# A delta-rule stage beside neighbourhood attention: diagonal blocks turned by TensorE, state update moved to ScalarE and GpSimd

## The reference, cut to what matters

```python
gamma = jnp.exp(jnp.where(lower, gc[..., :, None] - gc[..., None, :], -jnp.inf))
a_mat = jnp.where(strict, jnp.einsum('bhncd,bhnsd->bhncs', kb, k) * gamma, 0.0)
t_mat = a_mat + jnp.eye(C, dtype=f32)
u = triangular_solve(t_mat, v * beta[..., None], ...)
qk = jnp.einsum('bhncd,bhnsd->bhncs', q, k) * gamma
def step(S, inp):
    v_new = u_n - jnp.einsum('bhck,bhkv->bhcv', w_n, S)
    o = jnp.einsum('bhck,bhkv->bhcv', qd, S) + jnp.einsum('bhcs,bhsv->bhcv', qk_n, v_new)
    S = S * gl[..., None, None] + jnp.einsum('bhck,bhcv->bhkv', kd, v_new)
    return S, o
```

## Time and profile before

| | us |
|---|---|
| median of 3 runs | 3741.64 |
| lowest, highest | 3738.85, 3743.60 |
| the profiled execution | 3740.74 |
| its span | 3738.8 |
| TensorE busy in the span | 3666.4 |
| the delta stage, 371 to 720 us of the span | 349 |
| TensorE busy in that stage | 302.65 |

### The profile page before, as it was taken

One profiled execution on the slowest core, in us unless ns is written; L12 is line 12 of the kernel. 1 busy time (PEld: TensorE's weight loads), 2 busy tenths in 40 slices (PEclk: granted clock), 3 DMA queues, 4 the chain that ended last, 5 costly groups with the idle time before them and its releaser, 6 DMA issues.

```text
span 3738.8 us, 50657 instructions
## 1 busy us (share of the span) xinstructions
PE 3666.4 (98%) x21121; PEld 2968.1 (79%) x21121; DVE 2148.3 (57%) x3262; ACT 1579.8 (42%) x2544; POOL 81.4 (2%) x85
## 2 busy tenths in 40 slices
PE   8999888899999999999999999999999999999998
PEld 5887677778888878888788889888787788788887
DVE  5641678775345578757588564366655266555333
ACT  5451666634333444435353452333443333434333
POOL 0000121000000000000000000000000000000000
PEclk9999999999999999999999999999999999999999
DMA  5124321324322222222222222222222222223222
GB/s 198 46 74 107 83 58 40 116 91 108 111 91 95 94 81 80 90 96 91 89 80 91 94 93 85 91 85 84 81 95 92 94 85 81 83 92 117 96 96 85
DMA packets 118490, 340.27 MB, mean 91 GB/s; under 512 B 20072, under 2 KB 31864, under 8 KB 118136
## 3 DMA queue, kind: packets, MB, share of 16 engines
q1 hardware_dynamic: 116024, 331.52, 27.2%
q0 software_dynamic: 2240, 5.51, 0.7%
HBM read 318.47 MB, written 20.06 MB: 91 GB/s over the span
## 4 chain that ended last, share of the span: by engine, by line
PE 94%; DVE 3%; ACT 2%; issue 1%; DMA 0%; SPq 0%; ACTq 0%; DVEq 0%
PE ps L329 54%; PE ps L307 28%; PE ps L1324 1%; PE ps L808 1%; PE ps L2821 1%; PE ps L1032 1%; PE ps L1675 1%; PE ps L1642 1%; PE ps L1335 1%; DVE n_s L1764 1%; DVE g_D L1508 0%; PE ps L2250 0%; PE ps L2277 0%; ACT n_s L1709 0%; PE ps L2239 0%
## 5 line engine op out<-in xcount | busy, mean ns | idle before, releaser
L329 PE MATMUL ps<-a,w_hi 128*128 128x512 f32 (+1 forms) x6064 | 1837.9, 388 | 2.5 <-ACT l_vf L2657 0.8
L329 PEld LDWEIGHTS ps<-a,w_hi 128*128 128x128 f32 x6064 | 1110.0, 188 | 259.8 <-issue 10.6
L329 PE MATMUL ps<-a,w_lo 128*128 128x512 f32 (+1 forms) x3032 | 1147.2, 385 | 0.0
L268 DVE TENSOR_TENSOR w_lo<-w_raw,w_hi 128x1024 fp32r<-128x1024 f32 x539 | 657.9, 1221 | 396.9 <-ACT w_hi L263 394.1
L263 ACT ACTIVATE w_hi<-w_raw 128x1024 fp32r<-128x1024 f32 x539 | 563.6, 1050 | 516.2 <-DMA w_raw<-in_w_mlp 323.3
L329 PEld LDWEIGHTS ps<-a,w_lo 128*128 128x128 f32 x3032 | 562.6, 188 | 119.7
L307 PE MATMUL ps<-h_hi,w_hi 128*128 128x512 f32 x1528 | 485.5, 399 | 0.0
L307 PE MATMUL ps<-h_lo,w_hi 128*128 128x512 f32 x1528 | 478.9, 395 | 0.0
L307 PE MATMUL ps<-h_hi,w_lo 128*128 128x512 f32 x1528 | 478.8, 395 | 0.0
L374 DVE TENSOR_TENSOR h_lo<-u_sq,h_hi 128x512 fp32r<-128x512 f32 x192 | 132.9, 692 | 460.7 <-ACT h_hi L364 459.8
L390 DVE TENSOR_TENSOR xT<-xT,ps 128x1024 f32<-128x1024 f32 x191 | 232.9, 1219 | 247.2 <-PE ps L307 246.3
(11 more groups left out here) (392 smaller groups left out, 2959.6 us busy)
## 6 DMA issues: line engine op xcount, KB each, us to landing
w_raw<-in_w_mlp SPq DMA_DIRECT2D x384, 512.0 KB, 3.4
w_raw<-in_w_in SPq DMA_DIRECT2D x107, 512.0 KB, 3.4
w_raw<-in_w_out SPq DMA_DIRECT2D x48, 512.0 KB, 3.4
n_bias<-na_tab SPq DMA_DIRECT2D x36, 256.0 KB, 4.8
xT<-in_x SPq DMA_DIRECT2D x8, 512.0 KB, 8.7
x<-xT SPq DMA_DIRECT2D x2, 2048.0 KB, 8.3
g_row<-gate_rows SPq DMA_DIRECT2D x16, 256.0 KB, 3.2
xT<-x SPq DMA_DIRECT2D x2, 2048.0 KB, 11.2
```

Source lines behind the costliest of these rows:

```text
L268: nc.vector.tensor_tensor(w_lo[u.z][:, :], w_raw[u.z][:, :], w_hi[u.z][:, :].bitcast(F32), ALU.subtract).then_inc(w_split[u.z], 1)
L329: last = nc.tensor.matmul(ps[:, bank, 0:t1 - t0], w[:, k * P:(k + 1) * P], a[:, h, low, k, t0:t1], start=(i_k == 0 and i == 0), stop=(i_k ...
```

## The change

Five things change in the delta stage.

- The diagonal blocks of `g_A` are transposed by TensorE (`pairs_pe`): products of each 64x64 block with every second column of an identity, written to the bank that the key products left; they stand behind each direction's output products (and in `nv1_pe` for step 0). VectorE masks from that bank.
- VectorE's copies or additions of the output bank (`outputs`) stand behind level 1's mask in slot 1, not before level 1's transposes; those of the last step stay where they were.
- From step 1 on, GpSimd adds the per-head biases to `g_dec` and `g_qk` (4 more instructions), and ScalarE takes each exponential in one piece of 512 columns per direction.
- The state is updated by GpSimd: a multiplication per direction behind the output product, and an addition per direction of `g_up`, a copy of the increment that ScalarE makes in slot 1. L1535 goes.
- ScalarE takes the newer attention item first: its first two exponentials stand ahead of the copy of the folded output.

```diff
@@ nv1_pe
+                if end and at == 6:
+                    pairs_pe(pe, 0, 0)
             last.then_inc(mm_done[u.z], 1)
+            if end:
+                pairs_pe(pe, 0, 1)
...
+        def pairs_pe(pe, n, d):
+            pe.wait_ge(gs["A"], once(n, d))
+            for h in range(GH):
+                for i in range(2):
+                    part = side(i)
+                    last = nc.tensor.matmul(halves(stacked(gbank(d, 2)), 0, 1 - d)[part, h], g_A[d][part, h, part],
+                                            halves(const("fold").unsqueeze(1), 0, 1 - d)[part, 0], start=True, stop=True)
+            last.then_inc(gs["AT"], 1)
@@ first_level
-            dve.wait_ge(gs["A"], once(n, d))
-            for i in range(2):
-                ins = nc.vector.transpose(g_D[d][side(i), :, :], g_A[d][side(i), :, side(i)])
-            ins.then_inc(gs["AT"], 1)
-            yield
             dve.wait_ge(gs["AT"], once(n, d))
-            nc.vector.tensor_tensor(halves(g_gu[d][:, :, :], 0, 1 - d), halves(g_D[d][:, :, :], 0, 1 - d), lev_mask(0, d), ALU.mult)\
+            nc.vector.tensor_tensor(halves(g_gu[d][:, :, :], 0, 1 - d), halves(stacked(gbank(d, 2)), 0, 1 - d), lev_mask(0, d), ALU.mult)\
@@ exponents_act (factors_act alike, with g_qk and gs["dm"])
+            if n:
+                nc.scalar.activation(four(g_dec[d][:, :, :]), four(g_dec[d][:, :, :]), ACT.Exp).then_inc(gs["dec"], 1)
+                return
@@ gdn_pe, slot 0
                     step_out(m, 0)
+                    pairs_pe(pe, n, 0)
                     step_out(m, 1)
+                    pairs_pe(pe, n, 1)
@@ gdn_act
+                if s == 1 and 0 < n < TC:
+                    for d in range(2):
+                        act.wait_ge(gs["su"], once(m, d))
+                        nc.scalar.activation(four(g_up[d][:, :, :]), ps[:, gbank(d, 0), :], ACT.Copy).then_inc(gs["up"], 1)
@@ gdn_dve
-                if s == 0 and n:
-                    for d in both_ways(m):
...
+                if s == 0 and n == TC:
+                    outputs(m)
...
+                if s == 1 and 0 < n < TC:
+                    outputs(m)
...
-                if s in (2, 4) and 0 < n < TC:
-                    d = s // 2 - 1
-                    dve.wait_ge(gs["su"], once(m, d))
-                    dve.wait_ge(gs["S"], once(m, d))
-                    for h in range(GH):
-                        ins = nc.vector.scalar_tensor_tensor(g_S[d][:, h, :], g_S[d][:, h, :], gcol(G_LAST, m, d, h),
-                                                             pbank(gbank(d, 0))[:, h, :], op0=ALU.mult, op1=ALU.add)
-                    ins.then_inc(gs["S"], 1)
@@ gdn_pool
+                if n:
+                    for d in range(2):
+                        pool.wait_ge(gs["o"], once(m, d))
+                        pool.wait_ge(gs["S"], state_of(m, d))
+                        nc.gpsimd.tensor_tensor(g_S[d][:, :, :], g_S[d][:, :, :], gcols(G_LAST, m, d), ALU.mult).then_inc(gs["S"], 1)
+                    for d in range(2):
+                        pool.wait_ge(gs["S"], decayed_state(m, d))
+                        pool.wait_ge(gs["up"], moved(n, d))
+                        nc.gpsimd.tensor_tensor(g_S[d][:, :, :], g_S[d][:, :, :], g_up[d][:, :, :], ALU.add).then_inc(gs["S"], 1)
...
+                    for d in range(2):
+                        pool.wait_ge(gs["t1"], masked(n + 1, d))
+                        nc.gpsimd.tensor_tensor(g_dec[d][:, :, :], g_dec[d][:, :, :], gcols(G_CUMB, n + 1, d), ALU.add).then_inc(gs["t1"], 1)
+                    for d in range(2):
+                        q = factors_of(n + 1, d)
+                        pool.wait_ge(gs["t0"], masked(n + 1, d))
+                        nc.gpsimd.tensor_tensor(q, q, gcols(G_NCUM, n + 1, d), ALU.add).then_inc(gs["t0"], 1)
@@ na_act
-                for k, p in na_rows(i):
+                for k, p in reversed(na_rows(i)):
```

More of the change, by code:

```diff
@@ L1155, in build_program @@
         g_qk = both("g_qk", [P, 2, GH, P])
+        g_up = [work.take("g_up0", [P, GH, P]), Region(staged_at + 2048, staged_at + 4096).take("g_up1", [P, GH, P])]
         slots_at = [x_at + 4 * DC * T + 8 * UNIT * z for z in range(SLOTS)]
@@ L1296, in exponents_act, with masked, shifted, decayed_state @@
         def exponents_act(act, n, d):
+            if n:
+                nc.scalar.activation(four(g_dec[d][:, :, :]), four(g_dec[d][:, :, :]), ACT.Exp).then_inc(gs["dec"], 1)
+                return
             for h in range(GH):
-                t = (g_dec if n else g_dec0)[d][:, h, :]
-                ins = nc.scalar.activation(t, t, ACT.Exp, bias=gcol(G_CUMB, n, d, h))
+                ins = nc.scalar.activation(g_dec0[d][:, h, :], g_dec0[d][:, h, :], ACT.Exp, bias=gcol(G_CUMB, n, d, h))
             ins.then_inc(gs["dec"], 1)
+        def masked(n, d):
+            return 4 * n - 1 + d
+        def shifted(n, d):
+            return 4 * n + 1 + d
+        def decayed_state(m, d):
+            return 4 * m + 3 + d
+        def state_of(n, d):
+            return 4 * n + 1 + d
+        def moved(n, d):
+            return 2 * (n - 1) + d + 1
         def factors_of(n, d):
@@ L1306, in factors_act @@
         def factors_act(act, n, d):
+            if n:
+                nc.scalar.activation(four(factors_of(n, d)), four(factors_of(n, d)), ACT.Exp).then_inc(gs["dm"], 1)
+                return
             for h in range(GH):
@@ L1371, in state_keys @@
             def state_keys(n, d):
-                pe.wait_ge(gs["S"], once(n, d))
+                pe.wait_ge(gs["S"], state_of(n, d))
                 heads(gbank(d, 0), g_kT[:, :, toks(chunk_of(n, d))], g_S[d]).then_inc(gs["kS"], 1)
@@ L1438, in gdn_act @@
                     for d in range(2):
-                        act.wait_ge(gs["t0"], once(n, d))
+                        act.wait_ge(gs["t0"], shifted(n, d))
                         factors_act(act, n, d)
@@ L1466, in gdn_act @@
                     for d in range(2):
-                        act.wait_ge(gs["t1"], once(n + 1, d))
+                        act.wait_ge(gs["t1"], shifted(n + 1, d))
                         exponents_act(act, n + 1, d)
@@ L1479, in gdn_dve, with outputs @@
         def gdn_dve(dve):
+            def outputs(m):
+                for d in both_ways(m):
+                    dve.wait_ge(gs["o"], last_once(m, d))
+                    out = g_o[:, :, toks(chunk_of(m, d))]
+                    if m < TC // 2:
+                        nc.vector.tensor_copy(out, pbank(gbank(d, 1))).then_inc(gs["oe"], 1)
+                    else:
+                        dve.wait_ge(gs["oe"], TC)
+                        nc.vector.tensor_tensor(out, out, pbank(gbank(d, 1)), ALU.add).then_inc(gs["oe"], 1)
             unit_done(dve, nv1s[-1])
@@ L1488, in gdn_dve @@
                         pass
-                if s == 0 and n:
-                    for d in both_ways(m):
-                        dve.wait_ge(gs["o"], last_once(m, d))
-                        out = g_o[:, :, toks(chunk_of(m, d))]
-                        if m < TC // 2:
-                            nc.vector.tensor_copy(out, pbank(gbank(d, 1))).then_inc(gs["oe"], 1)
-                        else:
-                            dve.wait_ge(gs["oe"], TC)
-                            nc.vector.tensor_tensor(out, out, pbank(gbank(d, 1)), ALU.add).then_inc(gs["oe"], 1)
+                if s == 0 and n == TC:
+                    outputs(m)
                 if 1 <= s <= 12 and s % 2 and n >= 0:
@@ L1565, in gdn_pool @@
             for n in range(TC):
+                m = n - 1
+                if n:
+                    for d in range(2):
[6 more added lines that the diff above has]
+                        nc.gpsimd.tensor_tensor(g_S[d][:, :, :], g_S[d][:, :, :], g_up[d][:, :, :], ALU.add).then_inc(gs["S"], 1)
                 for d in range(2):
@@ L2005, in mixers_sp @@
                         sp.wait_ge(gs["eg"], once(n, d))
-                        sp.wait_ge(gs["t1"], once(n, d))
-                        sp.wait_ge(gs["t0"], once(n, d))
+                        sp.wait_ge(gs["t1"], masked(n, d))
+                        sp.wait_ge(gs["t0"], masked(n, d))
                     if n + 1 < TC:
@@ L2543, in build_program @@
         gl_old += [(na[name], ROWS) for name in ("neg", "inv", "sq", "ss", "z", "f", "of")]
[L2544 removed]
+        gl_old += [(gs["up"], 2 * (TC - 1))]
         gl = {name: old for name, (old, _) in zip(gl_names, gl_old)}
```

5 lines of the change are left out of this document (2 added, 3 removed).

## The result

| | us |
|---|---|
| changed kernel, median of 5 runs | 3758.37 (3755.56 to 3760.11) |
| ratio to before, 95% interval | 1.0045 (1.0035 to 1.0056) |
| predicted | 3747 (3733 to 3755) |
| its profiled execution | 3760.11, span 3758.2 (before 3740.74, span 3738.8) |

The change makes the kernel 16.7 us slower, three times the loss that was predicted, and outside the range. The loss lies in the delta stage: from the folded output's transposes of step 1 to those of step 8 the profile of after takes 307.1 us, before 290.3. That stretch begins 2.9 us later in after; 1.06 of it was there ahead of the first changed instruction (direction 1's key products of step 0 start at 376.08 and at 375.02), and 1.9 belongs to the start of the stage and step 0.

What follows compares the result with a forecast made beforehand. In the delta stage TensorE (busy 34.9 of 39.6 us a step), ScalarE and VectorE were taken to lead in turn. 1.2 + 0.0 + 4 x 0.87 + 0.65 + 0.0 = +5.3 us on the median 3741.64 gave 3747, range 3733 to 3755.

Steps and rivals of the forecast that it cites:

- a steady step: Delta-stage steps 2 to 5: engine terms of -0.78 us plus 1.65 of GpSimd waits, +0.87 us each.
- identity products: TensorE's gapless stretch before the folded output's transposes: 16 small products a step, +0.65 us, bounds 0.34 and 1.36.
- ScalarE -0.40: ScalarE's lead up to slot 3: two exponentials run earlier (-1.41), two increment copies come in (+1.0), -0.40 us a step.
- state -1.03: VectorE's lead in slot 4: the four state-update pieces of L1535 go, -1.03 us a step.
- the upper bound (1.36): Largest cost of TensorE's identity products, from L1347: two corners, 0.68 us for half as many products of twice the width.
- The waits, 1.65: VectorE's lead: L1779, L1783 and L1786 wait for GpSimd's bias additions, +1.65 us a step, bounds 0 and 3.7.
- r: L1779's wait on VectorE for the GpSimd addition in progress, between 0 and 1.2 us, taken as 0.6.
- rival C: Longer TensorE waits before slot 6 drop the clock in four more steps, 1.8 us each: +12.5, 3754; chance 0.20.
- B: VectorE's small instructions don't wait for GpSimd: -4.6 us, 3737; without half-clock stretches in steps 2 and 3, 3733.5; chance 0.28.
- A: Main case: all delta-stage terms as summed, including waits for GpSimd, +5.3 us, 3743 to 3751; chance 0.52.
- Start, +1.2: Start of the delta stage: direction 1's level 0 waits for identity products, mask and subtraction, first L1764 +1.2 us later.
- Steps 5 to 7: End of the delta stage: step 5 as a steady step, +0.87 us; step 6 +0.65; step 7 0.0.

Runs made afterwards that it cites:

- e4: Changed kernel with GpSimd's four bias additions waiting for slot 8's masked key-query products, so running in slots 9 to 12; 3744.54 us, ratio 1.0008.
- e9: Kernel before with only the two moves of order: output copies in slot 1, exponentials ahead of the folded output's copy; 3735.79 us, ratio 0.9982.
- e5: Changed kernel with transposes of g_A back on VectorE and biases back on ScalarE, keeping state update and both order moves; 3731.16 us, ratio 0.9975.
- e10: Kernel before with twelve additions a step added on GpSimd behind its own six instructions, results read by nothing; 3766.45 us, ratio 1.0064.
- e2: Changed kernel with the biases back in ScalarE's eight pieces of exponentials, no bias additions on GpSimd; 3738.68 us, ratio 0.9998.
- e15: Kernel before with the state update by ScalarE copies and GpSimd and output copies in slot 1, exponentials' order unchanged; 3746.05 us, ratio 1.0013.
- e6: Changed kernel with transposes of g_A and state update back on VectorE, keeping GpSimd's biases and both order moves; 3733.02 us, ratio 0.9981.
- e13: Kernel before with only ScalarE's exponentials moved ahead of its copy of the folded output; 3736.52 us, ratio 0.9984.

## Why the prediction was wrong

The direction and the mechanisms of the prediction held; two terms of a steady step were too small, that of the start too, and the clock's rival was given 0.20.

For steps 1 to 4 of the profiled runs (F to F, 162.2 us before, 171.7 after, +9.5) the rows give: leads 4 x -1.45 = -5.8; identity products 4 x 1.44 = +5.8; waits for GpSimd 4 x 2.24 = +9.0; clock +4.3 (steps 1, 2 and 4: 26.66, 26.65 and 26.48 against 25.18), less 3.5 that steps 2 and 3 had before. Sum +9.8, of 9.5 measured. The forecast for this stretch was 4 x 0.87 = +3.5, since the products of step 1 that it took as swallowed stand ahead of F. Of the 6.0 us between, identity products are 3.2, the waits 2.4 and the clock 0.8, which add up to 6.4.

The profiled executions differ by 19.4 us in all. Ahead of the stage they differ by 1.1; up to F of step 1 the change lost 1.9 (forecast 1.2 - 0.2 = 1.0), then 9.5 (3.5) and in steps 5 to 7 7.4 (0.8); behind that they differ by -0.4. The sum in the prediction had left out of step 7 its identity products and ScalarE's term (+0.65 - 0.40), which changes it by less than 0.3.

- **ScalarE -0.40 and state -1.03**: right. e4, free of waits, has 15.00 for before's 16.47. But e9 shows that -1.41 of it is the reversed order alone, and e5's first half is 15.00 with the state update on top, e9's 15.06: the state update gives nothing in a step at full clock. I had added up its credit and its cost without saying that they cancel.
- **Identity products, "I take 0.65, by the row of the same width"**: the failed step, a term of the sum that was sized too small. Measured +1.44 a step, over twice 0.65. TensorE's rows of step 4 place it: from the first output product to the second direction's first it takes 2.46 us for before's 1.83, from there to the increments 2.57 for 1.86, and the increments 1.89 for 1.79, so +0.63, +0.71 and +0.10. The rows of the products: 0.66 us for eight products of 32 columns on two corners (x16 records), 0.67 for sixteen on four corners (L1370, x32), and 0.63 for eight of 64 columns on two corners (L1382 in the same step, x16). Four products per corner take 0.6 us each time, with two corners or four, and with 32 columns or 64. The nearest row was L1347's, the upper bound (1.36), not the row of the same width. Over six steps the term was 4.7 us short. The Trainium skill, page "TensorEngine Tiling (Array Packing)", section "Instruction Overhead", would have given 0.80 as an estimate, 0.64 short of what was measured: here a small product cost 0.15 us of its corner's time.
- **The waits, 1.65**: right in kind and place, and in the time of L1779's successor (predicted F+11.4, measured 569.60, F+11.38); L1834 waited 0.91 (r had been put at 0.6), L1838 0.47 (0.8) and L1841 0.92 (0.25). Bias additions are 1.02 us long (two in 2.04), not 1.23, so the beat that I had laid over the three did not fit. A step lost 2.24; over six steps the term was 3.5 us short. This is the second term that failed. e4 moves only the time of GpSimd's additions, e10 adds only idle ones, and both show the waits. By the Trainium skill, page "SBUF — State Buffer", section "Who interferes with whom", a VectorE instruction with two SBUF inputs contends with a GpSimd instruction that reads SBUF; e2's rows beside after's (0.15 to 0.17 us against 1.06 and 1.07) agree for four columns too. The prediction's "the loser waits for the other's whole instruction" is too little for e10's 6.43 us.
- **L1773's successor** waited as well, which I had not forecast (L1828, with one SBUF operand, took up to 1.04 us where it otherwise took 0.17; at 596.48 it met the multiplication of `g_S` that GpSimd had begun at 596.45). Its exponentials come well ahead of F, so I count nothing for it; no run shows it apart.
- **The clock (rival C)**: after a wait of 1.69 ahead of slot 6's products TensorE ran at the lower level in the second half of steps 1, 2 and 4, not of step 3, whose wait was 1.69 too. In before's steps 2 and 3 it had fallen in the first half (18.58 and 18.91 us at PEclk 0.87 and 0.85), and there after has 1.00 in all four steps: so the stretches that B would have lost did go, and others came behind slot 7. That is C's kind of loss, at 1.3 to 1.5 us a time instead of 1.8. It came with A, not instead of it; the range's upper end, 3755, held C without the two short terms.
- **Start, +1.2**: right for the distance from the last value product to the first L1764 (2.30 to 3.48). But the first direction's products stand ahead of the last value products, and these now come 4.22 us behind the key products (376.08 to 380.30) and not 3.45 (375.02 to 378.47): +0.77, where 0.2 had been put. So the start cost 1.95.
- **Steps 5 to 7** lost 7.4 us where 0.8 was forecast. By the figures of steps 1 to 4, identity products are 2.9 (two gaps) and the leads -4.3. In step 5 the small instructions waited 2.3 us, in step 6 only L1838 did, 0.47, where 1.65 was forecast. In step 7 L1889 and L1892, the normalisations, took 1.59 and 1.64 us against 0.75 and 0.69 before; in step 6 they had met GpSimd in before already. That leaves about 4.2 us, with PEclk 0.83 to 0.94 in all six halves where before had 0.97 in the mean. How this rest splits is not settled.

Also open: what decides in which step the clock falls. e15 has it in the first half of steps 1 to 5 with the three small instructions free; after keeps full clock in step 3 with the same waits as in step 4. The experiments bound it: what is left of a difference when leads and waits are taken out is 1.2 us (e15) to 2.7 us (first half of step 1 of e6 and e9) for each half at lower clock; where it was 2.7, the half behind it was 0.5 us shorter.

## What to carry to other kernels

Before giving GpSimd work, lay its list in time against VectorE's instructions with SBUF operands alone, the tiny ones too: one of four columns can wait as long as the GpSimd instruction it meets lasts, or longer. Here either part alone cost nothing, and both together 13 to 15 us more than one, because the list then ended 15 us into the step and not 11. Where the work is wanted, try a wait that moves it past such a place: here one such line was worth 13.8 us (e4). Price small matrix products by rows that use the same corners of the array as often, not by rows of the same width. All rows here have four products per corner, so how the time goes with that number is not shown. When a bundle comes out neutral, try each edit alone: a pure reordering (e13, -4.9 us) was half of what the best kernel gained (e5, -10.0).
